# Latent attention without rotation matmuls: exchanged weight columns, earlier key signals, a later table wait, and weight splits moved ahead on ScalarE

## What is computed

```
q  = rms_norm(c_q) @ w_uq   -> 8 heads of 64 plain + 32 rotated components
kv = rms_norm(c_kv) @ w_ukv -> 8 heads of 64 plain key + 64 value components
q_rope = rotate(q[..., 64:], ang);  k_rope = rotate(k_r, ang)   # one k_r for all heads
rotate(x) = [x1*cos - x2*sin, x2*cos + x1*sin]                  # x1, x2: halves of 16
scores = (q_nope.k_nope + q_rope.k_rope) / sqrt(96); softmax over 256 keys; times v
```

## Time and profile before

| | |
|---|---|
| median of three runs | 2870.46 us (2867.01 to 2870.82) |
| the profiled execution | 2872.48 us, span 2870.7 us |
| busy: PE, DVE, ACT | 2617.0 us (91%), 1857.6 us (65%), 1496.9 us (52%) |
| bytes read | 581.73 MB, 203 GB/s over the span |
| mean granted clock of PE | 0.948 of full speed |

### The profile page before, as it was taken

How to read it: one execution, slowest core, us unless ns; L and a number is a source line. 1 busy time by engine, 2 the same in 40 slices (tenths; PEclk the granted TensorE clock), 3 DMA queues, 4 the chain that set the end, 5 groups by cost and what they waited for, 6 DMA issues and landing times.

```text
span 2870.7 us, 38623 instructions
## 1 busy us (share of the span) xinstructions
PE 2617.0 (91%) x16826; PEld 2329.6 (81%) x16826; DVE 1857.6 (65%) x1580; ACT 1496.9 (52%) x1442; POOL 0.2 (0%) x4
## 2 busy tenths in 40 slices
PE   6879999887899999999999997988799989878998
PEld 6769998766787878878787786877689988768998
DVE  4645445564688888888888885555565554546554
ACT  4244334433577777777776774445444444544443
POOL 0000000000000000000000000000000000000000
PEclk9879999997999999999999998999899999889999
DMA  5214554221499989989999894323145543223452
GB/s 203 89 59 146 178 190 149 101 89 59 177 366 349 368 348 360 355 347 367 348 364 351 352 358 169 133 89 133 44 162 180 189 145 118 83 94 116 149 191 89
DMA packets 83100, 585.32 MB, mean 204 GB/s; under 512 B 9481, under 2 KB 11209, under 8 KB 12273
## 3 DMA queue, kind: packets, MB, share of 16 engines
q1 hardware_dynamic: 82928, 582.81, 54.4%
HBM read 581.73 MB, written 1.05 MB: 203 GB/s over the span
## 4 chain that ended last, share of the span: by engine, by line
PE 82%; DVE 10%; ACT 6%; issue 1%; DMA 0%; ACTq 0%; SPq 0%; DVEq 0%
PE PS L1373 80%; ACT whi L500 2%; DVE wlo L843 2%; ACT pb L563 2%; PE PS L1757 1%; PE PS L1519 1%; ACT pt L579 1%; DVE hT L860 1%; DVE stat L938 1%; DVE pb L946 1%; DVE small L856 1%; DVE hT L911 0%; DVE pb L932 0%; DVE qe L1004 0%; DVE ke L1003 0%
## 5 line engine op out<-in xcount | busy, mean ns | idle before, releaser
L843 DVE TENSOR_TENSOR wlo<-raw,whi 128x2048 fp32r<-128x2048 f32 x550 | 1259.5, 2291 | 568.3 <-ACT whi L500 558.3
L500 ACT ACTIVATE whi<-raw 128x2048 fp32r<-128x2048 f32 x550 | 1051.9, 1913 | 375.5 <-PE PS L1373 374.6
L1373 PE MATMUL PS<-hhi,whi 128*128 128x256 f32 x1952 | 572.3, 293 | 31.9 <-DVE hlo L866 19.0
L1373 PE MATMUL PS<-hlo,whi 128*128 128x256 f32 x1952 | 563.3, 289 | 0.0
L1373 PE MATMUL PS<-hhi,wlo 128*128 128x256 f32 x1952 | 562.5, 288 | 0.0
L1373 PEld LDWEIGHTS PS<-hhi,whi 128*128 128x128 f32 x1952 | 384.9, 197 | 46.7 <-issue 40.4
L1373 PEld LDWEIGHTS PS<-hlo,whi 128*128 128x128 f32 x1952 | 385.9, 198 | 0.6 <-issue 0.5
L1373 PEld LDWEIGHTS PS<-hhi,wlo 128*128 128x128 f32 x1952 | 385.1, 197 | 0.0
L1373 PE MATMUL PS<-whi,xghi 128*128 128x512 f32 x896 | 360.1, 402 | 2.1 <-ACT pm L667 2.1
L1373 PE MATMUL PS<-whi,xglo 128*128 128x512 f32 x896 | 355.2, 396 | 0.0
L1373 PE MATMUL PS<-wlo,xghi 128*128 128x512 f32 x896 | 355.0, 396 | 0.0
(11 more groups left out here) (331 smaller groups left out, 3720.2 us busy)
## 6 DMA issues: line engine op xcount, KB each, us to landing
raw<-in_wm SPq DMA_DIRECT2D x336, 1024.0 KB, 4.9
raw<-in_ws SPq DMA_DIRECT2D x214, 1024.0 KB, 4.8
xT<-in_xT SPq DMA_DIRECT2D x1, 1024.0 KB, 4.8
bsum<-in_bsum SPq DMA_DIRECT2D x1, 1024.0 KB
out_T<-hT SPq DMA_DIRECT2D x4, 256.0 KB, 2.5
lmask<-in_lmask SPq DMA_DIRECT2D x1, 512.0 KB
tri<-in_tri SPq DMA_DIRECT2D x1, 256.0 KB
cmask<-in_cmask SPq DMA_DIRECT2D x1, 256.0 KB
```

The source lines that it names most:

```text
L500: act.activation(whi[s % SPLIT][:], raw[s % RAW][:], ACT.Copy).then_inc(hi_ready, 1)
L843: dve.tensor_tensor(wlo[s % SPLIT][:], raw[s % RAW][:], whi[s % SPLIT][:].bitcast(F32), ALU.subtract).then_inc(lo_ready, 1)
L1373: return pe.matmul(out, a, b, start=start, stop=stop, skip_group_check=True)
```

## The change

The weights of the latent query projection and of the shared key get 32 further output columns per head: the rotated components once more with their halves exchanged. Rows 96 to 127 of each projected head so hold the turned partners, and the sign is put into the sine table. The matmuls with `rotC` are gone. A new function `rope_c` on DVE reads both the rotated rows and the partners from PSUM, and multiplies with the scale as it goes, four heads at a time; ACT copies only the 64 plain rows. The queries go to banks 0 to 3, keys to 4 to 7, and the keys' matmuls signal by a semaphore of their own, `keys_done`, before the values' matmuls. PE and DVE wait for the tables only in front of the first rotation of the axial branch, where DVE also converts `selCT`; ACT doesn't wait for them. The calls of the table wait before the loop over the layers, of all three engines, and DVE's conversion there, are removed. In `attention` ACT's part of a filler is cut in two: the split (`split_ahead`) comes before the exponentials, the wait and the drain (`take_out`) come at the end of the iteration, behind the copy `pt`.

```diff
-TABLES2 = (..., "cosC", "sinC", "rotC", "selC", "selCT")
+TABLES2 = (..., "cosC", "sinC", "selC", "selCT")
...
+            def split_ahead():
+                return (fillers.pop(0), take()) if fillers else None
+            def take_out(filled):
+                if filled:
+                    f, used = filled
+                    act.wait_ge(unit_used, used)
+                    src = PS[:, 7, :] if f.wide is None else PS[:, 7, :].rearrange("p (t c) -> p t c", t=f.wide)
+                    act.activation(f.dst, src, f.func, scale=f.scale).then_inc(drained, 1)
+                    C.next(drained)
...
                 for n in range(len(jobs) + 2):
+                    filled = split_ahead() if n % fill_every == 0 else None
...
-                    if n % fill_every == 0:
-                        fill()
...
+                    take_out(filled)
...
-                    act.activation(qc[0:QW, 4 * i:4 * i + 4, :],
-                                   banks(4 + 2 * i, 2)...[0:QW, :, :], ACT.Copy,
+                    act.activation(qc[0:NOPE, 4 * i:4 * i + 4, :],
+                                   banks(2 * i, 2)...[0:NOPE, :, :], ACT.Copy,
                                    scale=QW ** -0.5).then_inc(drained, 1)
-                act.wait_ge(unit_used, take())
+                used = take()
+                after(keys_done)
                 act.activation(kc[0:NOPE, :, :], ...).then_inc(drained, 1)
+                act.wait_ge(unit_used, used)
                 act.activation(vc...).then_inc(drained, 1)
...
+            def rope_c(dst, src, turned_src, tmp, scale):
+                wide = lambda x: x.unsqueeze(1).to_broadcast([ROT, src.shape[1], S])
+                dve.scalar_tensor_tensor(out=tmp, in0=turned_src, scalar=scale, in1=wide(tables["sinC"][QW:P, :]),
+                                         op0=ALU.mult, op1=ALU.mult)
+                dve.scalar_tensor_tensor(out=dst, in0=src, scalar=scale, in1=wide(tables["cosC"][NOPE:QW, :]),
+                                         op0=ALU.mult, op1=ALU.mult).then_inc(rope_taken, 1)
+                C.next(rope_taken)
+                dve.wait_ge(rope_taken, C.now(rope_taken))
+                dve.tensor_tensor(dst, dst, tmp, ALU.add).then_inc(rope_done, 1)
...
+                if l == 0:
+                    after(tables_loaded, 16 * len(TABLES2))
+                    dve.tensor_copy(selCT[:], tables["selCT"][:]).then_inc(selectors_cast, 1)
                 rope(qa[:, 0:5, :], 5, P, "A", hT[:, 0:5, :])
...
-                rope(cc[0:QW, 5:6, :], 1, QW, "C", hT[0:QW, 0:1, :])
+                rope_c(cc[NOPE:QW, 5:6, :], cc[NOPE:QW, 5:6, :], cc[QW:P, 5:6, :], hT[NOPE:QW, 0:1, :], 1.0)
                 fill(len(fillers))
-                for i in range(3):
-                    take()
+                for i in range(2):
+                    dve.wait_ge(unit_used, take())
+                    hs, out = slice(4 * i, 4 * i + 4), banks(2 * i, 2).rearrange("p (h s) -> p h s", s=S)
+                    rope_c(qc[NOPE:QW, hs, :], out[NOPE:QW, :, :], out[QW:P, :, :], hT[NOPE:QW, hs, :], QW ** -0.5)
+                take()
                 C.next(drained, 4)
-                rope(qc[0:QW, :, :], NH, QW, "C", hT[0:QW, :, :])
...
+                if l == 0:
+                    after(tables_loaded, 16 * len(TABLES2))
+                    after(selectors_cast)
                 rope(qa[:, 0:5, :], 5, P, "A")
...
-                rope(cc[0:QW, 5:6, :], 1, QW, "C")
...
-                    claim(4 + 2 * i, 2)
+                    claim(2 * i, 2)
...
-                            cs = slice(h * QW, (h + 1) * QW)
-                            ins = mm3(out[0:QW, h, :], ...)
+                            cs = slice(h * P, (h + 1) * P)
+                            ins = mm3(out[:, h, :], ...)
                     ins.then_inc(unit_used, 1)
-                    empty(4 + 2 * i, 2, drained)
+                    empty(2 * i, 1, drained)
+                    empty(2 * i + 1, 1, rope_taken)
...
-                claim(0, 8)
+                claim(4, 4)
...
+                ins.then_inc(keys_done, 1)
+                claim(0, 2)
...
                 empty(4, 4, drained)
-                empty(0, 4, drained)
-                claim(0, 4)
-                rope(qc[0:QW, :, :], NH, QW, "C")
-                after(rope_done)
+                keys_out = C.now(drained)
+                empty(0, 2, drained)
+                after(rope_done, 3)
                 after(kr_ready)
+                pe.wait_ge(drained, keys_out)
                 attention(latent_heads(), pb2, pt2)
...
-                if l == 0:
-                    after(tables_loaded, 16 * len(TABLES2))
...
+    turn = c.pop("rotC").sum(0)[NOPE:QW, None]
+    c["sinC"] = np.concatenate([c["sinC"], turn * c["sinC"][NOPE:QW]])
...
+        lat[:, 640 + 96:640 + 112], lat[:, 640 + 112:] = w[:, 2960:2976], w[:, 2944:2960]
...
-        uq = k_units(inp["c_w_uq_2"][l], 384)
+        both = [h * QW + d for h in range(NH) for d in [*range(QW), *range(QW - ROT // 2, QW), *range(NOPE, QW - ROT // 2)]]
+        uq = k_units(inp["c_w_uq_2"][l][:, both], 512)
```

More of the change, by code:

```diff
@@ L71 @@
 TABLES1 = ("tri", "cmask", "bsum", "lmask", "onehot", "lbw")
-TABLES2 = ("cosA", "sinA", "rotA", "cosB", "sinB", "rotB", "cosC", "sinC", "rotC", "selC", "selCT")
+TABLES2 = ("cosA", "sinA", "rotA", "cosB", "sinB", "rotB", "cosC", "sinC", "selC", "selCT")
 class Count:
@@ L167, in build @@
             sem(n) for n in ("rope_turned", "rope_taken", "rope_done"))
+        keys_done = sem("keys_done")
         va_turned, va_ready, kr_ready, latent_hi, latent_ready = (
@@ L755, in second_mixer @@
                     act.wait_ge(unit_used, take())
-                    act.activation(qc[0:QW, 4 * i:4 * i + 4, :],
-                                   banks(4 + 2 * i, 2).rearrange("p (h s) -> p h s", s=S)[0:QW, :, :], ACT.Copy,
+                    act.activation(qc[0:NOPE, 4 * i:4 * i + 4, :],
+                                   banks(2 * i, 2).rearrange("p (h s) -> p h s", s=S)[0:NOPE, :, :], ACT.Copy,
                                    scale=QW ** -0.5).then_inc(drained, 1)
-                act.wait_ge(unit_used, take())
+                used = take()
+                after(keys_done)
                 act.activation(kc[0:NOPE, :, :], banks(4, 4).rearrange("p (h s) -> p h s", s=S)[0:NOPE, :, :],
                                ACT.Copy).then_inc(drained, 1)
+                act.wait_ge(unit_used, used)
                 act.activation(vc[:].rearrange("p t c -> p (t c)"), banks(0, 2), ACT.Copy).then_inc(drained, 1)
                 C.next(drained, 4)
-                C.next(rope_done)
+                C.next(rope_done, 2)
                 attention(latent_heads(), pb2, pt2)
@@ L914, in rope @@
                 dve.tensor_tensor(buf, buf, tmp, ALU.add).then_inc(rope_done, 1)
+                C.next(rope_done)
+            def rope_c(dst, src, turned_src, tmp, scale):
[7 more added lines that the diff above has]
+                dve.tensor_tensor(dst, dst, tmp, ALU.add).then_inc(rope_done, 1)
                 C.next(rope_done)
@@ L1344, in vector_program @@
                 norm(4 + 2 * l)
-                if l == 0:
-                    after(tables_loaded, 16 * len(TABLES2))
-                    dve.tensor_copy(selCT[:], tables["selCT"][:]).then_inc(selectors_cast, 1)
                 second_mixer(l)
@@ L1878, in second_mixer @@
                 head_norm(5, lambda t: tables["selC"][:, t, :], lambda t: selCT[:, t, :], 16, hT, [4, 5])
-                fill()
-                claim(0, 1)
-                rope(cc[0:QW, 5:6, :], 1, QW, "C")
-                C.next(rope_done)
                 fill(len(fillers))
+                C.next(rope_taken)
                 after(latent_ready)
@@ L1886, in second_mixer @@
                     w_hi, w_lo = take()
-                    claim(4 + 2 * i, 2)
-                    wh, wl = by_k(w_hi, 3, 4 * QW), by_k(w_lo, 3, 4 * QW)
-                    out = banks(4 + 2 * i, 2).rearrange("p (h s) -> p h s", s=S)
+                    claim(2 * i, 2)
+                    wh, wl = by_k(w_hi, 3, 4 * P), by_k(w_lo, 3, 4 * P)
+                    out = banks(2 * i, 2).rearrange("p (h s) -> p h s", s=S)
                     for h in range(4):
                         for k in range(3):
-                            cs = slice(h * QW, (h + 1) * QW)
-                            ins = mm3(out[0:QW, h, :], wh[:, k, cs], wl[:, k, cs], chi[:, k, :], clo[:, k, :],
+                            cs = slice(h * P, (h + 1) * P)
+                            ins = mm3(out[:, h, :], wh[:, k, cs], wl[:, k, cs], chi[:, k, :], clo[:, k, :],
                                       k == 0, k == 2)
                     ins.then_inc(unit_used, 1)
-                    empty(4 + 2 * i, 2, drained)
+                    empty(2 * i, 1, drained)
+                    empty(2 * i + 1, 1, rope_taken)
                 w_hi, w_lo = take()
                 wh, wl = by_k(w_hi, 2, UNIT // 2), by_k(w_lo, 2, UNIT // 2)
```

(10 more changed lines are left out.)

## The result

| | before | after |
|---|---|---|
| median, us | 2868.74 (2865.64 to 2870.82, 4 runs) | 2801.01 (2793.51 to 2802.76, 4 runs) |
| profiled execution, us | 2872.48 | 2802.39 |
| span, us | 2870.7 | 2800.6 |
| mean granted clock of PE | 0.948 | 0.956 |

A forecast was written before the change was run, and what follows sets the result against it. TensorE was taken to end 82% of the chain, with gains in the 16% it waits for VectorE and ScalarE; tables 3.8, latent 30.6, differential 19.8 and fox 9.0 sum to 63.2 us, giving 2807.3 us, range 2797 to 2827.

The forecast's parts named there:

- Tables: Before the first second mixer: TensorE starts projections without waiting for the selCT conversion, 3.8 us gained once.
- (a) to (d): Latent branch: no gap before keys, keys' copy hidden, no rotC matmuls, rotation beside matmuls; first scores 13.4 us earlier a layer.
- (e): Latent branch: after a shorter TensorE wait the first scores run fast, 1.89 instead of 3.79 us; 1.9 us a layer.
- Differential attention: whi ahead of exponentials, wlo beside them; 11.2 us per two jobs, 3.3 gained in each of three periods, 9.9 a layer.
- Fox attention: Two fillers: convolution 1.1 us earlier, scaling 3.4 to 3.5 earlier; 4.5 us a layer, table loads hidden by 0.7.
- Axial attention: TensorE sets the 9.12 us iteration either way: no gain; 0.1 us an iteration if the drain were twice as slow.
- (A): Rival: TensorE's clock replaces the chain, differential units start slowly, latent scores stay 3.79 us; gain 52.2, 2818 us; chance 0.12.
- (B): Rival: latent rope_c is late at 2.3 us an operation, fast scores lost too; gain 54.8, 2816 us; chance 0.04.
- (C): Rival: attention splits ahead gain little, something else holds VectorE; only tables and latent remain, 34.4 us, 2836; chance 0.05.
- (D): Rival: fox Silu table switches cost the skill's 2.66 us each; gain 59.2, 2811 us; chance 0.04.
- (E): Rival: slower, splits before attention exponentials wait for weight transfers; up to 125 us exposed, 2932 us; chance 0.03.
- over 7 us throughout: Sign of being wrong: TensorE's units in the attentions all take more than 7 us.

The follow-up runs named there:

- no splits ahead: Changed kernel with ScalarE's part of a filler back behind the exponentials in one piece; 2835.31 us, ratio to before 0.9871.
- early tables: Changed kernel with the table waits and the selCT conversion back in front of the norm; one run, 2806.41 us.
- drain first: Changed kernel with ScalarE's wait and drain of the filler back before the copy pt, split still ahead; one run, 2803.66 us.
- banks 2 and 3: Changed kernel with latent values in PSUM banks 2 and 3 and VectorE rotating before its second filler share; 2789.61 us, ratio to before 0.9718.
- old latent: Changed kernel with the rotC matmuls, 96-wide query weights and bank order of the kernel before; 2831.39 us, ratio to before 0.9869.
- keys late: Changed kernel with ScalarE copying the latent keys only when the whole keys and values unit is done; one run, 2801.89 us.
- slow rope: Changed kernel with two further VectorE products in front of each half of the latent queries' rotation; one run, 2809.56 us.

## Why the prediction was right, and where its sizes were off

**Tables:** right. 3.4 us by the stage, 3.5 by the experiment, 3.8 forecast; the 0.40 us conversion and its wait cost nothing in their new place, as the unchanged axial branch shows.

**Latent branch, (a) to (d):** right, 14.0 a layer instead of 13.4. Each part was seen: no gap at the keys, no `rotC` group, the wait ended by `vc`, six operations at 1.23 us (1.28 taken) hidden with 3.3 us to spare (3.7 taken). The keys' signal is worth 1.7 us of it, where the prediction priced its cover at 1.9. The 0.6 us more lie in the string of 132 matmuls: 19.38 us, where the prediction added up 11.25 + 8.65 and up to 0.15. The second query unit signals with its last matmul at 1970.59, which takes 0.28 us, so the scores start 9.65 us behind it, within the 9.6 to 9.9 of the forecast; keys and values take 8.45 us of that, 0.2 less than with the gap in front. ScalarE and VectorE at different rows of the same banks, for which no row stood, cost nothing in the 0.25 us in which they overlapped; a longer overlap wasn't seen.

**Latent branch, (e):** the term that was wrong. It priced fast first scores at 1.9 us a layer. They came (1.98 us), but the attention shortened by only 0.4 and 1.1 us, and even that can't be put down to them. All attentions without extra matmuls, of all kernels run here:

| first latent scores | kernels | attention, us | mean |
|---|---|---|---|
| fast, 1.9 to 2.0 us | after, no splits ahead, early tables, drain first, banks 2 and 3 | 25.93 to 29.27 (10) | 27.6 |
| slow, 3.8 us | before, old latent, keys late, slow rope | 26.65 to 28.69 (8) | 27.4 |

The step that failed is "so 1.9 us more", which took the clock of one group of matmuls for the clock of the stretch: over these 18 attentions fast first scores are worth nothing. The attention has gaps of its own, in which TensorE waits for VectorE and ScalarE, and the half level is granted somewhere in it. With fast first scores the gap in front of the first transposes is longer (3.04 us in each of the ten, 1.62 to 2.23 in the eight), and in layer 0 of the changed kernel the half level comes 1.5 us behind it. What goes with the time is the mean granted clock: 0.72 in the attention of 29.27 us, 0.77 and 0.81 in those of the changed kernel, 0.88 in those of 26.65, and 1.00 in all six with extra matmuls, which take 24.8 to 24.9. That the clock is the cost is shown; why a given gap brings the half level and another doesn't is not.

**Differential attention:** the mechanism was right, the term too small: 12.4 a layer, not 9.9. "I take 11.2" for the period was the mis-sized step; it is 10.6, which is VectorE's own sum in the prediction (10.6, about 10.7 with signals). The prediction let half of the units start slowly, as before (three of five did). Now only the first does (0.83 in its window, 1.00 behind it), and TensorE's largest gap in a period is 0.55 us. "Each of three periods" was the other step that didn't hold, as the table of periods shows: the first brings nothing, since TensorE's first unit, a slow one, ends the wait there, two bring 3.9 each, and 4.5 come behind the last, where the prediction had nothing. Of these, 2.2 are the clock alone (the last unit, 9.28 us before, 7.04 now). So 12.4 lies above the bound of 11.4 for this term, and that 3 x 3.9 would be near it is luck. The schedule laid by hand has 63.3 us for the old order, "which is what the trace shows"; the stage as cut here has 64.07. The clock was foreseen, as the extra 3 to 4 us in the range's lower end, but not in the sum. In no splits ahead it is at 0.87 again, so it follows from the chain.

**Fox attention:** 4.65 each, 4.5 forecast: 1.1 us up to the convolution and 3.55 behind it. That it agrees to 0.1 us is in part chance: of the 18 fox attentions with this code, in nine kernels, 5 take 36.9 us and 13 take 35.7 to 36.1, at a higher mean granted clock (0.86 or more instead of 0.79 to 0.82). The table loads are hidden by 0.7 us, as worked out. The Trainium skill, "ScalarE: Activation LUTs", section "What ACT_TABLE_LOAD costs", has 1.28 us for the load, which the rows agree with, and a drain of 1.38 us on top of it. No row has the drain: the Silu started 0.02 us after the load's end, at 161.31.

**Axial attention:** nothing, as forecast (87.86 to 87.82).

**Rivals.** (A) did not occur as it was put: the clock did not keep the differential attention slow, and the first latent scores were fast. It did take what (e) had counted on, a few matmuls later. (B) didn't occur; slow rope shows where it would begin. (C) is refuted by no splits ahead, 34.3 us. (D) is refuted by the rows. (E) didn't occur: no `whi` in the chain waits for a transfer. One of the signs of being wrong, units "over 7 us throughout", was badly drawn: a unit at the full clock takes 7.04 us.

**The rest.** The miss of 6.3 us (2807.3 against 2801.0) is this, in the traces: +5.0 differential, +1.2 latent up to the scores, +0.3 fox, -0.4 tables, -2.3 latent attention, +0.1 axial, and 3.0 from unchanged code, in sum 6.9; the medians of the runs differ by 0.6 from the profiled executions. The forecast is near in sum also because (e) and the differential attention erred in opposite directions. The 3.0 come from the stretch before the first fox attention, which no edit touches: it ends at 148.59 before and 144.24 after, 4.4 us earlier, and what else is outside the table gave some 1.3 back. The ten further kernels, with the same code up to there, have 144.73 to 148.42, so it differs from kernel to kernel or execution to execution, and these two are its ends: some 4 us of the 70 lie in code that the change doesn't touch. In it the same 48 matmuls began at the half clock in one trace and at the full clock in the other; here is the latter, from the timeline of TensorE of the changed kernel (before, the second took 0.42 us and stood behind a wait of 2.50):

```profile
54.30 0.39 PE L1397 MATMUL PS<-hhi,whi 128*128 128x256 f32 x1 [1.32 <-DVE wlo L854]
54.53 0.28 PE L1397 MATMUL PS<-hlo,whi 128*128 128x256 f32 x1
```

Of the 1.2 us by which that wait was longer, 0.7 are a `wlo` that was as much later, and 0.5 are matmuls in front of it that ended earlier. What moved those was not looked into.

## What to carry to other kernels

When two engines take turns on one chain, put the work of the one that needs nothing from the chain in front of the wait, not behind it: here the order of one split on ScalarE was worth 34 us of 68. When a chain of small waits gets short enough, TensorE's clock rises as a second gain; price both ends of it, and price the clock over a stretch, never for one group of matmuls. Look next at what the shorter chain leaves exposed: two banks of PSUM and one moved share of filler work gave another 10 us or so. And before a small gain is believed, look at the same stage in kernels in which its code is the same: here the two latent attentions of one kernel, with the same code, took 29.27 and 25.93 us.

## What the runs showed of the hardware

- Product and scaling from PSUM on VectorE cost by width, not by partitions, as far as these rows go: 32 x 1024 float32 took 1.23 us and 128 x 1024 from SBUF 1.28 us. For the shared key, 32 x 256 took 0.42 us and 96 x 256 in the kernel before 0.41.
- TensorE finished a stretch sooner when it was given 12 useless matmuls (24.86 us instead of 28.05 and 27.38; 24.8 to 24.9 in all six such attentions, 25.9 to 29.3 in the 18 without), as the granted clock stayed at its full level of 2.4 GHz instead of falling to 1.2 GHz in between. Seven such matmuls in another wait didn't keep it up: it fell 1.1 us after the first began (0.70 over their window). Behind them it was full, but the time of the stage stayed at 20.6 us.
- The local gain of 5.6 us (4.5 + 1.1) that such matmuls brought is not seen in the time of the whole kernel: 0.9728 [0.9712, 0.9743] with, 0.9718 [0.9705, 0.9731] without.
- The start of the same, unchanged code differs by up to 4.4 us between kernels (144.24 to 148.59), more than several of the effects above. The axial and differential stages agree within 0.1 us in the six kernels that have them as in the changed one; fox attentions with the same code differ by up to 1.2 us and latent ones by up to 3.3.
